# Per-head recurrence matrices kept compact (128x64) and multiplied as 64x64 tiles, both token tiles interleaved

## The reference

```
sa    = state @ (-kk_t)
state = state * w_t + sa (kk_t * a_t)^T + v_t k_t^T
y_t   = state @ r_t
```

```python
def wkv7_scan(r, decay, k, v, kk, a):
    ...
    def step(state, inp):
        r_t, w_t, k_t, v_t, kk_t, a_t = inp
        sa = jnp.einsum('bhvk,bhk->bhv', state, -kk_t)
        state = (state * w_t[:, :, None, :]
                 + sa[..., None] * (kk_t * a_t)[:, :, None, :]
                 + v_t[..., None] * k_t[:, :, None, :])
        return state, jnp.einsum('bhvk,bhk->bhv', state, r_t)
```

## Time and profile before

| | us |
|---|---|
| median of three executions | 1188.09 |
| span of the profiled execution, first to last instruction | 1185.6 |
| recurrence, first gram to the head mean (149.87 to 271.57) | 121.7 |
| TensorE busy over the span | 1107.6 (93%) |
| weight stream of the experts, from about 815 us | the DMA queues end each wait |

### The profile page before, as it was taken

One profiled execution on the slowest core, in us unless ns is written; L12 is line 12 of the kernel. 1 busy time (PEld: TensorE's weight loads), 2 busy tenths in 40 slices (PEclk: granted clock), 3 DMA queues, 4 the chain that ended last, 5 costly groups with the idle time before them and its releaser, 6 DMA issues.

```text
span 1185.6 us, 16275 instructions
## 1 busy us (share of the span) xinstructions
PE 1107.6 (93%) x6737; PEld 765.0 (65%) x6737; DVE 484.6 (41%) x708; ACT 357.8 (30%) x506; POOL 41.6 (4%) x34
## 2 busy tenths in 40 slices
PE   6999999999999999999999999999989989898986
PEld 5996778778997999987798654434343434242422
DVE  4774143544576353446664743222222212121212
ACT  5742311115455344345554231101111101010102
POOL 0003200000020101100000000000000000000000
PEclk9999999999999999999998999999999999999999
DMA  9445246232363655555436687999999999999994
GB/s 325 167 173 177 74 148 212 73 141 72 142 213 112 209 183 173 184 207 212 142 138 214 258 365 286 419 419 420 421 420 420 420 420 420 421 421 420 420 421 201
DMA packets 95055, 316.69 MB, mean 267 GB/s; under 512 B 7879, under 2 KB 32791, under 8 KB 70295
## 3 DMA queue, kind: packets, MB, share of 16 engines
q1 hardware_dynamic: 93958, 313.19, 68.3%
q10 hardware_dynamic: 1040, 2.69, 0.6%
HBM read 314.81 MB, written 1.05 MB: 266 GB/s over the span
## 4 chain that ended last, share of the span: by engine, by line
PE 72%; DMA 20%; DVE 5%; ACT 2%; issue 1%; SPq 0%; POOL 0%; DVEq 0%; ACTq 0%
DMA arena<-in_w 19%; PE bank L1420 11%; PE bank L756 11%; PE bank L758 11%; PE bank L757 11%; PE bank L987 5%; PE bank L1444 4%; PE bank L742 4%; PE bank L916 2%; PE bank L1400 1%; PE bank L943 1%; PE bank L733 1%; PE bank L1457 1%; PE bank L703 1%; DVE arena L2275 1%
## 5 line engine op out<-in xcount | busy, mean ns | idle before, releaser
L1420 PE MATMUL bank<-ring,hT 128*64 128x512 f32 x512 | 227.0, 595 | 29.5 <-DMA arena<-in_w 28.4
L1420 PE MATMUL bank<-arena,hT 128*64 128x512 f32 x512 | 227.0, 595 | 0.0
L758 PE MATMUL bank<-h_high,ring_low 128*128 128x256 f32 x688 | 194.4, 283 | 0.0
L1420 PEld LDWEIGHTS bank<-ring,hT 128*64 128x64 f32 x512 | 67.8, 137 | 182.0 <-issue 130.8
L553 DVE TENSOR_TENSOR ring_low<-ring,hi_high 128x2048 fp32r<-128x2048 f32 (+2 forms) x58 | 126.1, 2219 | 102.1 <-ACT hi_high L1591 102.1
L756 PE MATMUL bank<-h_high,hi_high 128*128 128x256 f32 x528 | 148.6, 281 | 0.7 <-DVE h_low L2098 0.7
L757 PE MATMUL bank<-h_low,hi_high 128*128 128x256 f32 x528 | 148.0, 280 | 0.0
L1591 ACT ACTIVATE hi_high<-ring 128x2048 fp32r<-128x2048 f32 (+2 forms) x58 | 104.5, 1855 | 90.5 <-DMA ring<-in_w_ffn_up 35.5
L758 PEld LDWEIGHTS bank<-h_high,ring_low 128*128 128x128 f32 x688 | 131.3, 191 | 0.0
L1444 PE MATMUL bank<-arena 128*64 128x512 f32 x384 | 113.3, 596 | 7.1 <-DVE hT L2702 6.6
L2708 DVE TENSOR_TENSOR arena<-arena,bank 128x512 f32<-128x512 f32 x16 | 17.3, 1083 | 230.7 <-ACT arena L1948 230.7
(11 more groups left out here) (408 smaller groups left out, 1781.5 us busy)
## 6 DMA issues: line engine op xcount, KB each, us to landing
arena<-in_w SPq DMA_DIRECT2D x112, 1024.0 KB, 23.0
ring<-in_w SPq DMA_DIRECT2D x80, 1024.0 KB, 20.5
ring<-in_w_in SPq DMA_DIRECT2D x15, 2048.0 KB, 7.9
ring<-in_w_ada SPq DMA_DIRECT2D x12, 2048.0 KB, 8.3
ring<-in_w_ffn_gate SPq DMA_DIRECT2D x11, 1024.0 KB, 5.3
ring<-in_w_ffn_up SPq DMA_DIRECT2D x11, 1024.0 KB, 7.9
ring<-in_w_ffn_down SPq DMA_DIRECT2D x5, 2048.0 KB, 7.8
ring<-in_w_o SPq DMA_DIRECT2D x2, 2048.0 KB, 7.6
```

What stands on the lines that cost most here:

```text
L758: return mm(ps, a[1], b[0], start=False, stop=stop)
L1420: last = mm(both(6 + half, x), hg[:, k, (2 * q + x) * CAP:(2 * q + x + 1) * CAP], w13s[x][k // 4][:, k % 4, half * EF:(half + 1) * EF], st ...
```

## The change

The zeros are dropped. A pair of 64x64 chunk blocks is now stored side by side in the partitions, as 128 partitions by 64 columns (chunk 0 in partitions 0 to 63, chunk 1 in 64 to 127), so all buffers of that form are half as wide; what this frees holds both token tiles at once. Each 128x128 matmul of a group becomes two 64x64 matmuls, one in the upper left and one in the lower right quarter of the array. The work of the two token tiles is interleaved: every stage and every level is done for four groups `(i, q)` before the next stage. `ada` now stands in every level (eight calls as before). The products across chunks and heads use all four quarters (`CROSS`). The two chunks of `ry` and `y` get a bank each, and the masks that zeroed the off-diagonal blocks of `psi` and `phi` go away.

```diff
-            chunk = 1
-            for i in range(NT):
-                for h in range(HEADS):
-                    o, p = DH * (h % 2), h // 2
-                    ps = write(pe, ("g", i, h))
-                    right = kr[o:o + DH, p, i, :, :].rearrange("p s t -> p (s t)")
-                    mm(ps[:, 0:2 * P], bh[o:o + DH, p, i * P:(i + 1) * P], right, start=True, stop=True)
-                    mm(ps[:, 2 * P:4 * P], kh[o:o + DH, p, i * P:(i + 1) * P], right, ...).then_inc(...)
-                def group(key, q, left, right):
-                    ps = write(pe, key)
-                    for j in range(4):
-                        last = mm(ps[:, j * P:(j + 1) * P], left(4 * q + j), right(4 * q + j), start=True, stop=True)
-                    last.then_inc(*full(key))
...
+            half = [slice(CH * c, CH * c + CH) for c in range(2)]
+            both = [(i, q) for i in range(NT) for q in range(2)]
+            CROSS = ((0, 0), (1, 1), (0, 1), (1, 0))
+            def grams(i, q):
+                ps = [write(pe, ("g", i, q, e)) for e in range(2)]
+                for a in range(2):
+                    p = 2 * q + a
+                    for n, src in enumerate((bh, kh)):
+                        for e, c in CROSS:
+                            w = slice(4 * CH * a + 2 * CH * n, 4 * CH * a + 2 * CH * (n + 1))
+                            last = mm(ps[e][half[c], w].rearrange("s (x t) -> s x t", x=2),
+                                      src[half[e], p, i * P + CH * c:i * P + CH * (c + 1)],
+                                      kr[half[e], p, i, :, half[c]], start=True, stop=True)
...
+            def group(key, q, left, right, w=CH):
+                ps = write(pe, key)
+                for j in range(4):
+                    for r in half:
+                        last = mm(ps[r, j * w:(j + 1) * w], left(4 * q + j, r), right(4 * q + j, r), start=True, stop=True)
+                last.then_inc(*full(key))
+            for i, q in both:
+                grams(i, q)
+            ada(1)
+            for i, q in both:
...
+                group(("n", i, q), q, lambda h, r: gm[r, i, h, 0:CH], lambda h, r: K("eye")[r, :])
+            for lv in range(1, LEVELS):
+                for i, q in both:
...
+                    group(("x", i, lv, q), q, lambda h, r: gm[r, i, h, 0:CH], lambda h, r: dd[r, i, h, :])
+                ada(lv + 1)
+                for i, q in both:
+                    drained(pe, ("x", i, lv, q))
+                    if lv < LEVELS - 1:
+                        group(("d", i, lv, q), q, lambda h, r: ddT[r, i, h, :], lambda h, r: xx[r, i, h, :])
+                    group(("dt", i, lv, q), q, lambda h, r: xx[r, i, h, :], lambda h, r: ddT[r, i, h, :])
...
+            for i, q in both:
+                group(("w1", i, q), q, lambda h, r: gm[r, i, h, 2 * CH:3 * CH], lambda h, r: vp[r, i, h, :])
+            ada(LEVELS + 1)
+            for i, q in both:
...
+                group(("u", i, q), q, lambda h, r: ddT[r, i, h, :], lambda h, r: zb[r, i, h, :], P)
+            ada(LEVELS + 2)
...
+            def ry_of(i):
+                ps = [write(pe, ("ry", i, c)) for c in range(2)]
+                for p in range(PAIRS):
+                    for c, e in CROSS:
+                        h = 2 * p + e
+                        last = mm(ps[c][half[e], at(p)], tk[half[c], i, h, :], gm[half[c], i, h, CH:2 * CH], ...)
...
+            ry_of(0); psi_of(0, 1); phi_of(1); ry_of(1); psi_of(2); phi_of(2)
+            y_inside(0); state(1); y_before(1); y_inside(1); state(2); y_before(2); y_before(3)
```

(The last two lines stand one call to a line in the code.) `psi_of` is 16 matmuls of 64x64 by 64 columns per chunk, `phi_of` 8, `y_inside` 16 per chunk, `state` and `y_before` 8 each, `ry_of` 16 per token tile. On the readers' side:

```diff
-                    V.tensor_tensor(gm[:, h, :], ps[:, :], K("gram_mask"), ALU.mult).then_inc(*free(("g", i, h)))
+            for i, q in both:
+                for e in range(2):
+                    ps = filled(dve, ("g", i, q, e))
+                    V.tensor_tensor(gm[:, i, 4 * q + e:4 * q + 4:2, :], ps[:, :].rearrange(...), gram_mask, ALU.mult)...
...
+            for lv in range(1, LEVELS):
+                ada_sum(ADA_EARLY[lv])
+                for i, q in both:
+                    ...
+                    if lv < LEVELS - 1:
+                        V.copy_predicated(dd[:, i, hs, :], lmask(lv, 0), four(ps)).then_inc(*free(("d", i, lv, q)))
+                    V.copy_predicated(ddT[:, i, hs, :], lmask(lv, 1), four(ps)).then_inc(*free(("dt", i, lv, q)))
...
-                    V.tensor_tensor(psi[:, k], heads4(ps), blocks, ALU.mult).then_inc(*free(("psi", k)))
+                V.tensor_copy(psi[:, k], four(ps)).then_inc(*free(("psi", k)))
-                V.tensor_tensor(phi[:, k - 1], heads4(ps), blocks, ALU.mult).then_inc(*free(("phi", k)))
...
+                for p in range(PAIRS):
+                    ins = V.scalar_tensor_tensor(phi[:, k - 1, p, :], K("eye"), pc[...], ps[:, p * CH:(p + 1) * CH],
+                                                 ALU.mult, ALU.add)
```

More of the change, by code:

```diff
@@ L1040, in phi_of @@
[L1040 to L1057, removed]
@@ new lines, in psi_of @@
+            def psi_of(*chunks):
+                ps = {k: write(pe, ("psi", k)) for k in chunks}
+                for p in range(PAIRS):
+                    for n in range(2):
+                        for c, e in CROSS:
+                            for k in chunks:
+                                if k % 2 == c:
+                                    i, h = k // 2, 2 * p + e
+                                    left, right = ((btok, up[half[c], i, h, :]), (ktok, vp[half[c], i, h, :]))[n]
+                                    last = mm(ps[k][half[e], at(p)], left[half[c], i, h * DH:(h + 1) * DH], right,
+                                              start=(n == 0), stop=(n == 1))
+                                    if p == PAIRS - 1 and n == 1 and (c, e) in CROSS[2:]:
+                                        last.then_inc(*full(("psi", k)))
@@ new lines, in y_inside @@
+            def y_inside(i):
+                for c in range(2):
+                    ps = write(pe, ("y", i, c))
+                    for p in range(PAIRS):
+                        for n in range(2):
+                            for e in range(2):
+                                h = 2 * p + e
+                                left, n0 = ((up, CH), (vp, 3 * CH))[n]
+                                last = mm(ps[half[e], at(p)], left[half[c], i, h, :], gm[half[c], i, h, n0:n0 + CH],
+                                          start=(p == 0 and n == 0), stop=False, skip_group_check=True)
+                    last.then_inc(*(full(("y", i, c)) if (i, c) == (0, 0) else (S("y_inside"), 1)))
@@ new lines, in y_before @@
+            def y_before(k):
+                i, c = k // 2, k % 2
+                pe.wait_ge(S("y_inside"), k)
+                drained(pe, ("ry", i, c))
+                drained(pe, ("psi", 0) if k == 1 else ("s", k - 1))
+                ps = bank[BANK["y", i, c][0]]
+                for p in range(PAIRS):
+                    for r in half:
+                        last = mm(ps[r, at(p)], psi[r, k - 1, p, :], ryT[r, p, k * CH:(k + 1) * CH], start=False,
+                                  stop=True, skip_group_check=True)
+                last.then_inc(*full(("y", i, c)))
@@ L1090, in _ @@
+            ry_of(0)
+            psi_of(0, 1)
+            phi_of(1)
+            ry_of(1)
+            psi_of(2)
+            phi_of(2)
+            y_inside(0)
+            state(1)
+            y_before(1)
+            y_inside(1)
+            state(2)
+            y_before(2)
+            y_before(3)
             for i in range(NT):
-                drained(pe, ("y", i))
+                for c in range(2):
+                    drained(pe, ("y", i, c))
             for j in range(2):
@@ L2314, in _ @@
+            state_out(2)
             for c in (2, 3):
```

309 lines of the change are left out of this document (134 added, 175 removed).

## The result

The kernel with the change took 1151.83 us (median of five executions, 1146.18 to 1153.53), the kernel before 1187.49 us beside it: a ratio of 0.970, with an interval of 0.967 to 0.972. Two more series of five, on other chips, gave 0.967 (0.9645 to 0.9693) and 0.967 (0.9648 to 0.9693). So the change gains 36 to 40 us. The forecast was 1141.5 us and a gain of 46.6. The profiled executions of the other two series took 1152.07 and 1150.37 us.

What follows compares the result with a forecast made beforehand. The prediction took the number and length of TensorE instructions to bound the kernel. Recurrence terms 8.3 + 4.4 + 40.0 + 9.4 + 13.0 = 75.1 us, against 121.7, gave a forecast of 1141.5 us, range 1131 to 1158.

Steps and rivals of the forecast that it cites:

- grams and `ada(1)`: Start of the recurrence: 128 gram instructions in 5.7 us, between two and four at a time, then `ada(1)` 2.6; 8.3 us.
- n and level 1's x: Group n and first x: DVE binds with eight merges, 3.0 us; with first group, last x and handovers 4.4 us.
- levels: Five levels of groups at 0.51 us plus `ada` at about 2.67: 6.8, three of 8.8, and 6.8; 40.0 us together.
- w1, `ada`, u, last sum: After the levels: four w1 groups at 0.51, `ada` 2.67, four `u` groups at 0.94, last sum 0.86; 9.4 us.
- tail to the head mean: Recurrence's end from `ry` on: 400 instructions in 11.8 us, DVE wait about 0.5, final copy and mean 0.73; 13.0 us.
- The price of a pair: Two 64x64 instructions in opposite quarters overlap at 64 ns per pair, so a group takes 0.51 us, not 0.94.
- The second rival: Pairs in one PSUM bank run one after another, 128 ns each: 12.7 us slower, 1200.8 us; chance 0.07.
- DVE's merges: In n and the levels, each DVE merge of 256 columns costs 0.38 us, with bounds 0.29 and 0.61.
- the sum: The terms of the whole recurrence add up to 75.1 us against 121.7, 46.6 less.
- the cover: In each level DVE's eight merges, 3.0 us, fit under 4.1 us of TensorE work; ACT's copies are hidden too.
- Rival 3: Small tiles or waits bring the clock down in the recurrence's last part, which doubles: + 13, 1154 us; chance 0.07.
- DMA: Weight loads in the recurrence land in 8.3 us, a slot lost every 8.8: no wait, else at most some 3 us.

Runs made afterwards that it cites:

- e1: The change with the lower right half of every call of group left out, so half of group's instructions go: 1143.5 us, ratio 0.963.
- e2: The change with both instructions of each pair in the upper left quarter (chunk 0 computed twice): 1173.2 us, ratio 0.988.
- e3: The change with only 256 KB of 2 MB loaded for five chunks of modulation weights during the recurrence: 1142.1 us, ratio 0.962.
- e4: The change with each 2 MB load in the recurrence cut into four, each but the first waiting for a TensorE group: 1144.0 us, again 1144.8.
- e8: e4 with the parts of the last two loads started earlier, under `u`: 1140.9 us, ratio 0.962.
- e9: e8 with the parts of the first two paced loads also started later: 1140.3 us, ratio 0.962.
- e5: e4 with the first gate matmuls after the recurrence moved in two halves into its tail: 1148.8 us, ratio 0.968.

## Why the prediction was right, and where it was short

Its steps, by their terms (us):

| step | forecast | measured |
|---|---|---|
| grams and `ada(1)` | 8.3 | 6.5 |
| n and level 1's x | 4.4 | 5.1 |
| levels | 40.0 | 47.2 |
| w1, `ada`, u, last sum | 9.4 | 9.6 |
| tail to the head mean | 13.0 | 14.2 |
| recurrence | 75.1 | 82.6 |

- **The price of a pair** was right in mechanism and near in size: 58 ns measured from start to start, 64 forecast, a group 0.48 us instead of 0.51. e1 and e2 show both halves of the argument, the price of a tile alone and the free second one. The 52 groups of the levels gained 1.7 us on the forecast.
- **The second rival** rested on a rule of the Trainium skill ("TensorEngine Tiling (Array Packing)", Gotcha 1: PSUM Pressure), that different row tiles can't access the same PSUM bank simultaneously. The trace does not bear it out for this case: the two row tiles of L990 write one bank, in different partitions, and start 7 ns apart, at 58 ns a pair. The measurement decides.
- **The grams** run four at a time: 128 instructions in 3.65 us, 28.5 ns each, just under the lower bound of the forecast (3.8 us). The same holds in the tail for `psi` (L1052): 64 instructions in 0.93 us.
- **DVE's merges** were slightly cheaper than forecast, 0.33 us apart:

```profile
157.08 0.43 DVE L2307 COPY_PREDICATED arena<-lvl,bank 128x256 f32<-128x256 uint8 x1
157.41 0.44 DVE L2310 COPY_PREDICATED arena<-lvl,arena 128x256 f32<-128x256 uint8 x1
```

  So the wait of 1.0 us before the rest of level 1's x is a block end, not DVE; in e3, without it, n and x took 4.29 us, where the sum has 4.4.
- **The levels** are the step that failed, in "the cover": no wait of DVE or ACT came, as forecast, but block waits, which the sum didn't have. They cost 4.7 us: 0.4 and 3.4 within the groups, and 0.9 in the fourth `ada`, whose 16 instructions of L911 took 2.71 instead of 1.85 us because the block ended behind the third of them. The half clock cost 3.4 us, and each `ada` 0.2 more than forecast (0.98 or 1.06 + 1.85), 1.0 in all. Less the 1.7 us of the groups this is about the 7.2 us that is missing.
- **Rival 3** had the clock, but in the last part and with + 13. In the first series it fell in level 2, for 6.8 us; in the other two also in the tail (at 224.6 and 221.8 us, 6.9 us long). The argument against it, that the change leaves no wait of that length, was wrong: waits of 3.3 and 2.2 us came.
- **The tail**: the streams were about 2.5 us shorter than forecast, the wait for DVE before `y_before(3)` was 0.6 us (0.5 forecast), and 3.7 us of block waits came on top. I had looked only at DVE.
- **DMA** "no wait" was right for the weights and wrong for the step as a whole: the load was weighed against the time of its own reader, not against the other user of the same queues, TensorE's instruction stream.
- **Luck** had a part. The block waits and the half clock cost 13 us, and the recurrence is only 7.5 us over the sum, because the other terms were priced some 5 us too high (grams 1.8, groups of the levels 1.7, streams of the tail 2.5, less 1.0 for `ada`). So the 75.7 us with light loads and 74.5 to 75.3 with paced ones, which look like the sum of 75.1, still hold 2.4 to 5.3 us of block waits and in e3 3.4 us by the half clock; without them they would be near 70.

The clock also explains most of the spread between executions. The record has span and mean clock of each, and the span times what the clock lacks of 1 is an estimate of the loss, if TensorE were always what the program waits for. In the first series the spans are 1144.4, 1150.0, 1151.4, 1151.7 and 1147.8 us at 0.991, 0.986, 0.984, 0.984 and 0.990; less the loss they are 1134.1, 1133.9, 1133.0, 1133.3 and 1136.3. The median of the spans so corrected is 1132.3 and 1132.5 us in the other series of the change, 1127.3 to 1128.3 in e3 and e4, 1128.4 and 1129.2 in e8 and e9, and 1171.6 to 1173.4 before. By this estimate spreading or leaving out loads gains 3 to 5 us, about what the block waits shrink by. The loss by the clock (median 13 us before, 14 to 16 in the change, 14 in e4, 9 to 10 in e8 and e9) lies mostly outside the recurrence, and that the paced loads lower it is not shown.

What stays open: whether a block wait makes the clock fall. It fell behind some, and it also fell with TensorE at work all along, in e1 and in the kernel before (at 57.2 and 309.7 us, where it was busy for 7.2 and 7.7 us without a gap). Reading the moved gate result earlier on ACT, which e5 lacks, was not tried.

## What to carry to other kernels

Splitting a block-diagonal matmul into two 64x64 ones in opposite quarters doubled the pace here, but it also gives four times the instructions per us: price the instruction stream as a transfer, with a time of its own per 256 instructions, and look at what else its queues carry at that time. When the profile shows a TensorE wait called "issue" in the middle of a group, count all of TensorE's instructions, semaphore waits too, to the last such wait; if the distances are multiples of 256, spread the loads or put long instructions there, and before moving work into such a gap, ask which bank and which reader it then waits for.

## What the runs showed of the hardware

- TensorE's program came in blocks of 256 instructions. Behind a wait and with idle queues the next block was usable 3.7 and 4.1 us after the present one began (the change, at 220.90 and 224.56); with weights at 250 to 400 GB/s blocks that ended in a wait took 5.3 to 7.2 us (three profiles of the change).
- Four quarters at once: 14.6 ns per 64x64 instruction (L1038, L1052), two at once 29 ns, one alone 58 to 60 ns.
- Two tiles in different rows and columns of the array wrote one PSUM bank, in different partitions, fully overlapped (L990: 58 ns a pair, starts 7 ns apart).
- The clock was at half for 6.8 us after waits of 3.3 us (the change) and 2.2 us (e3), but stayed at full after another wait of 2.2 us (the change, at 218.70). In e4, e8 and e9, whose longest waits were 2.0, 1.0 and 0.8 us, it stayed at full through the recurrence. In e1 it fell with TensorE at work all along, with mostly one quarter of the array in use, and in the kernel before, at 57.2 and 309.7 us, mostly with tiles of 128x128 in use.
